# A seventh pair of weight halves and a longer lead for the conversions in a two-block transformer kernel

## What is computed

```python
x = x + 0.5 * swiglu(rms_norm(x), wg, wu, wd)          # D_FF = 2816
x = x + mixer(rms_norm(x) @ w_in) @ w_out              # retention, attention, convolution
x = x + 0.5 * swiglu(rms_norm(x), wg, wu, wd)
```

## Time and profile before

| | us |
|---|---|
| median of three runs | 2198.03 |
| the profiled execution's own time | 2196.24 |
| its span, first to last instruction | 2194.4 |
| TensorE busy / VectorE busy / ScalarE busy / GpSimd busy | 2175.4 / 1515.8 / 1116.1 / 25.8 |
| share of the span: chain of work that ended last, on TensorE / VectorE / ScalarE | 91% / 6% / 2% |
| bytes read, mean rate | 460 MB, 210 GB/s |

### The profile page before, as it was taken

How to read it: one execution, slowest core, us unless ns; L and a number is a source line. 1 busy time by engine, 2 the same in 40 slices (tenths; PEclk the granted TensorE clock), 3 DMA queues, 4 the chain that set the end, 5 groups by cost and what they waited for, 6 DMA issues and landing times.

```text
span 2194.4 us, 26673 instructions
## 1 busy us (share of the span) xinstructions
PE 2175.4 (99%) x10710; PEld 1818.6 (83%) x10710; DVE 1515.8 (69%) x2313; ACT 1116.1 (51%) x1735; POOL 25.8 (1%) x32
## 2 busy tenths in 40 slices
PE   8999999999999999999999999999999999999998
PEld 7888888888888888888888987888888889778887
DVE  5655974456875977877876555888688766558565
ACT  5445654444445654445445666544454456655443
POOL 0000010000000010000000000000000000000000
PEclk9999999999999999999999999999999999999999
DMA  8554454556884457876876444688768864445653
GB/s 300 193 199 149 151 181 172 192 199 216 284 299 157 158 184 267 282 258 208 280 277 215 144 150 134 201 272 276 267 226 285 285 198 157 145 136 186 226 201 125
DMA packets 252800, 462.91 MB, mean 211 GB/s; under 512 B 11958, under 2 KB 58080, under 8 KB 252548
## 3 DMA queue, kind: packets, MB, share of 16 engines
q1 hardware_dynamic: 252276, 460.85, 62.0%
q10 hardware_dynamic: 400, 0.36, 0.1%
HBM read 460.12 MB, written 1.05 MB: 210 GB/s over the span
## 4 chain that ended last, share of the span: by engine, by line
PE 91%; DVE 6%; ACT 2%; issue 0%; DMA 0%; POOL 0%; SPq 0%; POOLq 0%; DVEq 0%; ACTq 0%
PE ps L1894 18%; PE ps L1897 18%; PE ps L1895 18%; PE s L1894 8%; PE s L1897 8%; PE s L1895 8%; PE ps L1864 4%; DVE wl L2544 2%; DVE cacc L2772 1%; PE s L2042 1%; PE ps L1910 1%; PE ps L1908 1%; PE ps L1909 1%; PE ps L2068 1%; DVE gts L2945 1%; ACT pt L2342 1%
## 5 line engine op out<-in xcount | busy, mean ns | idle before, releaser
L2544 DVE TENSOR_TENSOR wl<-raw,wh 128x1024 fp32r<-128x1024 f32 (+2 forms) x740 | 856.1, 1186 | 132.3 <-ACT wh L2235 128.2
L2235 ACT ACTIVATE wh<-raw 128x1024 fp32r<-128x1024 f32 (+2 forms) x740 | 731.6, 1031 | 393.1 <-PE ps L1897 127.1
L1894 PE MATMUL ps<-wh,xh 128*128 128x512 f32 (+3 forms) x1600 | 615.0, 384 | 0.4 <-DVE wl L2544 0.4
L1897 PE MATMUL ps<-wh,xl 128*128 128x512 f32 (+3 forms) x1600 | 604.2, 378 | 0.1
L1895 PE MATMUL ps<-wl,xh 128*128 128x512 f32 (+3 forms) x1600 | 603.9, 377 | 0.0
L1894 PEld LDWEIGHTS ps<-wh,xh 128*128 128x128 f32 x1600 | 300.8, 188 | 57.1 <-issue 9.7
L1897 PEld LDWEIGHTS ps<-wh,xl 128*128 128x128 f32 x1600 | 300.5, 188 | 48.8 <-DVE xl L2589 0.5
L1895 PEld LDWEIGHTS ps<-wl,xh 128*128 128x128 f32 x1600 | 301.0, 188 | 45.5
L2552 DVE SCALAR_TENSOR_TENSOR acc<-raw,condT,acc 128x512 f32<-128x512 f32 x252 | 188.8, 749 | 5.1
L2335 ACT ACTIVATE hTh<-ps 128x512 fp32r<-128x512 f32 x88 | 48.3, 596 | 219.0 <-PE ps L1864 219.0
L2696 DVE TENSOR_TENSOR hTl<-ps,hTh 128x512 fp32r<-128x512 f32 x88 | 57.1, 687 | 139.9 <-ACT hTh L2335 139.8
(11 more groups left out here) (370 smaller groups left out, 2426.7 us busy)
## 6 DMA issues: line engine op xcount, KB each, us to landing
raw<-in_ffn_w_in SPq DMA_DIRECT2D x80, 1024.0 KB, 5.4
raw<-in_ada_w SPq DMA_DIRECT2D x72, 1024.0 KB, 6.0
raw<-in_ffn_wu SPq DMA_DIRECT2D x40, 1024.0 KB, 5.8
raw<-in_ffn_wd SPq DMA_DIRECT2D x40, 1024.0 KB, 5.5
raw<-in_ffn_w_out SPq DMA_DIRECT2D x40, 1024.0 KB, 6.1
raw<-in_ffn_wg SPq DMA_DIRECT2D x39, 1024.0 KB, 5.3
raw<-in_mix_w_in SPq DMA_DIRECT2D x28, 1024.0 KB, 5.2
raw<-in_w_in SPq DMA_DIRECT2D x28, 768.0 KB, 4.5
```

The costliest lines, as they stand in the source:

```text
L1894: e.matmul(o, X[0](kk, t), hi, start=kk == 0, stop=False)
L1897: ins = e.matmul(o, X[1](kk, t), hi, start=False, stop=kk == K - 1 or (banks[t], kk) == self.closed)
L2235: ins = self.e.activation(m.wh[j % NH][:, 0:n], m.raw[u % NR][:, k0 * w:k0 * w + n], ACT.Copy)
L2544: ins = self.e.tensor_tensor(m.wl[j % NH][:, 0:n], m.raw[u % NR][:, k0 * w:k0 * w + n], hi, ALU.subtract)
```

## The change

It sets NH to 7 and the two depths to (5, 0) and (6, 1); `NH - TAIL` becomes 4 by this. It takes GpSimd's `split_lo_pool` out with its semaphore. In `skewed`, all four subs are brought up with `ahead(4, 0)` at the start, wh and wl, and `first_hi` runs all four wl products beside the wh products; `first_wl` is gone.

```diff
-NH = 6
-FFN_DEPTH, MIX_DEPTH = (3, 0), (4, 1)
+NH = 7
+FFN_DEPTH, MIX_DEPTH = (5, 0), (6, 1)
...
     def skewed(self, label, banks):
...
-        while self.wsub < self.taken + 4:
-            self.make()
+        self.ahead(4, 0)
         b0, b1 = self.next_t(), self.next_t()
         two = nx[0] == "final"
         v0 = self.turn_scaled(s, 0, ((b0, 0), (4, 0), (b1, 0), (b1, 256)), two)
-        if len(self.later) > 1:
-            self.lower(pool=True)
...
-        js = [self.take(label, i < 3) for i in range(4)]
-        x = lambda k: self.shh(s, 0, k)
-        early = range(NH - 3)
-        self.first_hi(js, banks[0], x, early)
+        js = [self.take(label) for _ in range(4)]
+        self.first_hi(js, banks[0], lambda k: self.shh(s, 0, k))
         self.shifted_lo(s, 0, 2)
         self.shifted_lo(s, 0, 3)
-        for i in range(len(early), 3):
-            self.first_wl(js, banks[0], x, i)
         self.first_lo(js, banks[0], s, (2, 3), False)
         v1 = self.turn_scaled(s, 1, ((5, 0), (5, 256), (b0, 0), (b0, 256)), two)
-        while self.later:
-            self.lower()
         for p in range(2):
             self.shifted_lo(s, 0, p)
-        self.first_wl(js, banks[0], x, 3)
         self.first_lo(js, banks[0], s, (0, 1), True)
...
                 k = 2 * i + n
                 self.wait_ge((self.s.hi, j), x(k))
                 e.matmul(o, X[0](k, 0), m.wh[hs][:, n * w:(n + 1) * w], start=k == 0, stop=False)
-                if i in early:
-                    self.wait_ge(self.lo_at[j])
-                    e.matmul(o, X[0](k, 0), m.wl[hs][:, n * w:(n + 1) * w], start=False, stop=False)
+                self.wait_ge(self.lo_at[j])
+                e.matmul(o, X[0](k, 0), m.wl[hs][:, n * w:(n + 1) * w], start=False, stop=False)
```

More of the change, by code:

```diff
@@ L379, in __init__ @@
         self.lo, self.vec = (Sem(sem(n), "DVE") for n in ("s_lo", "s_vec"))
-        self.pow, self.plo = (Sem(sem(n), "POOL") for n in ("s_pow", "s_plo"))
+        self.pow = Sem(sem("s_pow"), "POOL")
         self.raw = [Landed(sem(f"s_raw{i}")) for i in range(NR)]
@@ L435, in __init__ @@
         self.half = None
-        self.rows_scaled = None
         self.closed = None
@@ L533, in split_sums, with lower @@
             self.reduces.append((q, self.taken))
-    def lower(self, pool=False):
+    def lower(self):
         j, u, k0, nk, w, last = self.later.pop(0)
[L538 to L543, removed]
+        self.lo_at[j] = (self.s.lo, j)
+        self.split_lo(j, u, k0, nk, w)
         if last:
@@ L550, in split_lo @@
     def split_lo(self, j, u, k0, nk, w):
-        pass
-    def split_lo_pool(self, j, u, k0, nk, w):
         pass
@@ L792, in turn_scaled @@
         for h in range(2):
-            self.rows_scaled = (self.s.vec, ("xs", s, t, h))
             self.scale_rows(s, t, h, two)
@@ L897, in skewed, with first_hi @@
         return self.s.sub, js[-1][0]
-    def first_hi(self, js, b, x, early):
-        pass
-    def first_wl(self, js, b, x, i):
+    def first_hi(self, js, b, x):
         pass
@@ L2958 @@
     engine = "POOL"
[L2960 to L2966, removed]
     def scale_part(self, t, n, summed, done):
```

## The result

The changed kernel takes 2208.74 us (median of four runs, 2208.43 to 2210.07) against 2198.11 us for the kernel before on the same chip: ratio 1.0054, 95% interval 1.0042 to 1.0066. It is 0.5% slower. The prediction said 2196.2 us and no change; both the time and the sign were wrong. The profiled execution's span is 2206.7 us, 12.3 us more than before; between the medians it is 10.6 us.

What follows compares the result with a forecast made beforehand. TensorE, at 99% of the span, was taken as the bound, never waiting for weight halves in mid-stage. Gains of 1.3 + 0.4 = 1.7, say 1.8 us, gave 2196.2 us, counted as no change; range 2191.8 to 2200.

Steps and rivals of the forecast that it cites:

- Lead of five in the feed-forwards: Feed-forwards: loads issued some two subs earlier, same count of instructions and DMAs, subs between never waited; taken as 0.
- In-order blocking: Rival, feed-forwards with ada units: ScalarE, held by earlier-requested w_in loads, delays work behind them; slower, 2206 us, chance 0.08.
- The fourth wl in the skewed starts: Skewed starts: making this wl with the tail gains 0.84 us in the first, 0.23 in third and sixth; 1.3 us.
- The first bound by the second start: First skewed start: its stretch to `first_rest` shrinks from 7.51 us to the second start's 6.67, a gain of 0.84 us.
- Lead of six in the mixers: End of the second block's mixers: TensorE's wait at the merged rows' transposes goes, 0.22 us twice, 0.4 us gained.
- The bounds for the first block's mixers: First block's mixers: possible losses of up to 0.8 us each from ScalarE's burst and 0.6 us from wider wl.
- GpSimd's wl at 0: Removing GpSimd's wl path costs and saves nothing, since all 740 wl stand on VectorE.
- the new pair at 0: The seventh pair moves later tiles by 8 KB; no instruction's time goes by its address, so 0.
- The wait moves: Rival, skewed starts: ScalarE's vT or xh, 0.45 us later, holds `first_rest` instead; no gain, 2198.0 us, chance 0.17.
- more than the seams: Rival, mixers: stalls on the softmax chain go too, 6.2 us gained in all, 2191.8 us, chance 0.13.
- The even gap is a buffer gap: Rival, all matmuls: 0.2265 us spacing comes from too few buffers; more pairs give 117 us less, 2081 us, chance 0.01.

Runs made afterwards that it cites:

- depth4_early: Changed kernel with a feed-forward lead of 4 instead of 5 and the first sum of each feed-forward falling four subs earlier: 2207.46 us.
- late_sums: Changed kernel, leads 5 and 6 kept, with each flush in a feed-forward asking two subs more of age, so sums fall as before or later: 2197.47 us.
- nr5_nh6: Changed kernel with six pairs of weight halves instead of seven and five raw buffers instead of four, leads kept: 2237.3 us.
- seven_only: Changed kernel with the leads of before, (3, 0) and (4, 1): keeps 1.0 us at the first start, loses 0.69 and 0.74 us at third and sixth.
- mix_old: Changed kernel with only the mixers' lead back at 4, the feed-forwards keeping 5: 2209.8 us.

## Why the prediction was wrong

*The step that failed* is "Lead of five in the feed-forwards ... so I take 0". Its cover, that the subs never wait for a half in mid-stage, held: in the changed kernel the one wait for a wl (0.7 us) stands at the second sub, as before (0.4 us), and matmuls are 0.2265 us apart. But the step counted only weight halves. It held that "the count of instructions and of DMAs is the same", and did not ask whether their *order on TensorE* was. The due times are in the code and the sums' matmuls in the trace; TensorE's order around a seam, read against the last mac, gave 9.8 to 10.7 us of room, and the shift of a due time by four subs costs 10.9. Measured: +12.4 us at three sums.

*In-order blocking*, the slower rival at 0.08, priced at 2206, came nearest in time and was right about the place (feed-forwards with ada units) and about TensorE waiting for the ada sums. Its mechanism was a minor part: of the 12.1 us of room lost behind the third start, a later mac is 0.3 us and the order the rest. Against a lead of four it is more, 1.4 us of the wait (depth4_early). late_sums takes the waits away with the blocking left in: ScalarE waits 3.07 and 4.75 us for w_in in it at the third start, and no sum is late:

```profile
1420.14 2.01 ACT L2204 ACTIVATE wh<-raw 128x1024 fp32r<-128x1024 f32 x2 [3.07 <-DMA raw<-in_ffn_w_in]
1426.90 1.06 ACT L2204 ACTIVATE wh<-raw 128x1024 fp32r<-128x1024 f32 x1 [4.75 <-DMA raw<-in_ffn_w_in]
```

Only together with the early place did late loads make the long waits there (nr5_nh6).

*The fourth wl in the skewed starts*: forecast 0.84 + 2 x 0.23 = 1.3 us. Measured 1.04, 0.45 and 0.44, and 0.2 at each of the three others: 2.6 us. The first bound by the second start was right to 0.2 us. What it missed is that this holds for the third and sixth only together with the longer mixer lead (seven_only).

*Lead of six in the mixers*: the forecast 0.22 us twice was 0.32 and 0.31. The step stopped there; the burst that it moved out of the stretch before comes back in the next loop, ahead of `yl`, and costs 1.17 us twice. "What is late next" was asked for zt, not for yl. The bounds for the first block's mixers (0.8 and 0.6 us each) were not needed: no step there.

*GpSimd's wl at 0 and the new pair at 0*: no run speaks against it. *The wait moves* and *more than the seams*: the starts gained more, and no softmax stall went away. *The even gap is a buffer gap*: refuted. With seven pairs and any of the leads tried the distance is 0.2265 us and the busy share of weight loads is 82 to 83%; that share, which the Trainium skill's Perfetto Trace Analysis (Identifying Performance Opportunities) offers as a measure of headroom, pointed to none that buffers can give here.

*The range* ended at 2200.0 since it added small bounds of steps that were looked at, and had nothing for an order that shifts.

What stays open: why behind the first start the mac is no earlier, where no late load was shown to matter; the price of an early sum with a fifth raw buffer beside seven pairs, which was not tried; and why the lower clock follows some waits of some 2 us and not others.

## What to carry to other kernels

When a due time is written as an age since the issue of something, every change of a lead moves it against the other engines: list what falls elsewhere in the in-order queue of the bounding engine, and take its room at the worst place, right behind a seam, where the lead has been spent. Where a lead is lengthened, find where the catch-up burst falls and which small, urgent instruction stands behind it. A standstill of TensorE of two to three us is to be priced with what the clock may take afterwards.

## What the runs showed of the hardware

A standstill of TensorE can cost half as much again through the clock. In the changed kernel both waits of over 3 us (3.21 and 3.28) are followed by matmuls 0.427 us apart for about 3.5 us; the wait of 2.22 us is not:

```profile
1011.95 0.39 PE L1875 MATMUL ps<-wh,xl 128*128 128x512 f32 x1
1014.56 0.66 PE L1842 MATMUL ps<-cst,acc 128*128 128x128 f32 x4 [2.22 <-DVE acc L2521]
1014.97 0.48 PE L1872 MATMUL ps<-wh,xh 128*128 128x512 f32 x1
1015.28 0.39 PE L1873 MATMUL ps<-wl,xh 128*128 128x512 f32 x1
1015.51 0.39 PE L1875 MATMUL ps<-wh,xl 128*128 128x512 f32 x1
```

It is no clean line by the wait's length. In mix_old the wait of 2.22 us at sub 350 is not followed by slow matmuls either, but a shorter one of 2.13 us at sub 552 is, with a granted clock of 0.51 from 1633.2 to 1636.7:

```profile
1632.52 0.50 PE L1917 MATMUL ps<-ach,onesr 128*128 128x512 f32 x1 [2.13 <-DVE acl L2528]
1633.84 0.63 PE L1875 MATMUL s<-wh,xl 128*128 128x512 f32 x1
1634.27 0.63 PE L1872 MATMUL s<-wh,xh 128*128 128x512 f32 x1
```

And depth4_early's other executions show less clock than its profiled one for the same program. The prediction had no term for this in any rival.
